# w2 of a mixture-of-experts layer read in runs of 16 KB, its up product at a stride of four, up weights loaded whole

## What is computed

```
h = silu(xb @ w1[e]) * (xb @ w3[e])
out += ((h @ w2[e]) * gate)[rows of the tokens]
```

## Time and profile before

| | before |
|---|---|
| median of 3 runs | 1159.68 us (1159.65 to 1160.03) |
| profiled execution | 1160.26 us |
| its span in the trace | 1158.3 us |
| PE busy | 1002.4 us (87%) |
| DVE busy | 533.9 us (46%) |
| ACT busy | 400.9 us (35%) |
| POOL busy | 273.3 us (24%) |
| moved by DMA | 308.96 MB, mean 267 GB/s |
| weights rawe, 1024 KB loads | 128, median 20.7 us to landing |
| weights rawe, 2048 KB loads | 32, median 25.7 us to landing |

### The profile page before, as it was taken

One profiled execution on the slowest core, in us unless ns is written; L12 is line 12 of the kernel. 1 busy time (PEld: TensorE's weight loads), 2 busy tenths in 40 slices (PEclk: granted clock), 3 DMA queues, 4 the chain that ended last, 5 costly groups with the idle time before them and its releaser, 6 DMA issues. The chain is left out here.

```text
span 1158.3 us, 24709 instructions
## 1 busy us (share of the span) xinstructions
PE 1002.4 (87%) x9068; PEld 695.8 (60%) x9068; DVE 533.9 (46%) x983; ACT 400.9 (35%) x713; POOL 273.3 (24%) x319
## 2 busy tenths in 40 slices
PE   5999999999998999999994789989898888677460
PEld 4888888888886666788884445545454444333230
DVE  5741522111017888655457644352534343434338
ACT  5412233212125667303213334252343434242322
POOL 0101010101000000000000346464555454614120
PEclk9999999999999999999996799999999999989795
DMA  8733331531324004537549999999999999999986
GB/s 317 285 124 119 118 127 45 209 144 45 145 78 169 1 1 146 162 116 308 220 180 401 404 403 414 414 416 414 413 412 414 415 415 413 415 417 415 416 356 244
DMA packets 78645, 308.96 MB, mean 267 GB/s; under 512 B 9400, under 2 KB 9576, under 8 KB 62224
## 3 DMA queue, kind: packets, MB, share of 16 engines
q1 hardware_dynamic: 66224, 273.87, 60.0%
q0 software_dynamic: 12384, 34.63, 7.7%
HBM read 275.68 MB, written 36.44 MB: 269 GB/s over the span
## 5 line engine op out<-in xcount | busy, mean ns | idle before, releaser
L620 PE MATMUL ps<-whi,xTh 128*128 128x512 f32 x480 | 187.6, 391 | 13.9 <-DVE wlo L1283 13.9
L622 PE MATMUL ps<-whi,xTl 128*128 128x512 f32 x480 | 187.5, 391 | 0.0
L621 PE MATMUL ps<-wlo,xTh 128*128 128x512 f32 x480 | 187.5, 391 | 0.0
L915 PE MATMUL ps<-cur13a,xT 128*32 128x256 f32 x1984 | 133.8, 415 | 3.4 <-issue 2.2
L915 PE MATMUL ps<-cur13b,xT 128*32 128x256 f32 x1984 | 121.1, 385 | 13.4 <-DVEq L1780 13.4
L939 PE MATMUL ps<-cur,hT 128*32 128x256 f32 x1952 | 117.9, 382 | 7.5 <-issue 7.5
L1769 DVE COPY cur13a<-rawe 128x4096 f32 x31 | 71.2, 2296 | 112.9 <-DMA rawe<-in_w 63.3
L1017 ACT ACTIVATE zst<-ps,rstd 128x512 f32<-128x512 f32 x60 | 40.8, 688 | 205.0 <-PE ps L622 202.9
L1898 POOL DMA_INDIRECT y_scratch<-ystage,idxs x62 | 88.7, 1431 | 97.0 <-ACT ystage L1225 72.8
L1246 ACT ACTIVATE cur<-rawe 128x4096 f32 x30 | 108.7, 3622 | 8.4 <-issue 7.7
L620 PEld LDWEIGHTS ps<-whi,xTh 128*128 128x128 f32 x480 | 90.6, 189 | 32.7 <-issue 13.9
(11 more groups left out here) (238 smaller groups left out, 1362.4 us busy)
## 6 DMA issues: line engine op xcount, KB each, us to landing
rawe<-in_w SPq DMA_DIRECT2D x128, 1024.0 KB, 20.7
rawe<-in_w SPq DMA_DIRECT2D x32, 2048.0 KB, 25.7
raw<-in_w_in SPq DMA_DIRECT2D x20, 1024.0 KB, 8.0
z_scratch<-zst POOLq DMA_DIRECT2D x60, 256.0 KB, 2.3
gat<-z_scratch SPq DMA_DIRECT2D x12, 512.0 KB, 3.9
xn_scratch<-rrow POOLq DMA_DIRECT2D x6, 1024.0 KB, 5.7
raw<-in_w_out SPq DMA_DIRECT2D x4, 1024.0 KB, 6.7
xcol<-in_x_cols SPq DMA_DIRECT2D x6, 512.0 KB, 10.2
```

The lines of the kernel that those rows point to most:

```text
L620: pe.matmul(out, ah, bh, start=first, stop=False)
L621: pe.matmul(out, ah, bl, start=False, stop=False)
L622: return pe.matmul(out, al, bh, start=False, stop=last)
L915: mm = pe.matmul(ps[0][u * CAP:(u + 1) * CAP, 0:256], xT[:, c % 2, x:x + CAP], cur13[h][:, :, c * 512 + u * P:c * 512 + (u + 1) * P], star ...
```

## The change

w2 is dealt to the partitions as w1 and w3 are: partition p takes the four neighbouring rows 4p to 4p + 3, one run of 16 KB. The hidden units have to follow: chunk u of the hidden must hold the units u, u + 4, u + 8 and so on. So column tile u of the up product reads every fourth column of the weights from column u on, at a stride of four elements (16 bytes), where it read 128 neighbouring ones.

The halves of w1 and w3 are no longer loaded by themselves. Each of the two matrices comes in one load of 2 MB, w1 with `s_w1` and w3 with `s_w3`, and they lie in the slot one after the other, 16 KB each. SP waits until both halves of the slot are copied out, issues w1 and w3, waits for the copy of w2 and issues w2: three loads an expert, where there were five. DVE waits for w1 and w3 ahead of the first copy. A copy still takes half h of both, now from two pieces 16 KB apart in the slot. The hand-issued loads at the start follow, with w1 whole where half 0 of w1 and w3 was.

```diff
--- before.py
+++ after.py
@@ -341,8 +341,8 @@
         s_tbm = sem("s_tbm")
         s_ic = sem("s_ic")
         s_nb = sem("s_nb")
-        s_wa = [sem(f"s_wa{s}") for s in range(RING)]
-        s_wb = [sem(f"s_wb{s}") for s in range(RING)]
+        s_w1 = [sem(f"s_w1{s}") for s in range(RING)]
+        s_w3 = [sem(f"s_w3{s}") for s in range(RING)]
         s_w2 = [sem(f"s_w2{s}") for s in range(RING)]
         s_c13 = sem("s_c13")
         s_cw2 = sem("s_cw2")
@@ -384,7 +384,7 @@
         w_out = A["w_out"][0].rearrange("(p c) n -> p c n", c=KC)
         w_pab = [A[n][0].rearrange("(h p) n -> p h n", p=P) for n in ("w_pa", "w_pb")]
         e_w = [A[n][0].rearrange("e (p h c) f -> e p h (c f)", h=2, p=P) for n in ("w1", "w3")]
-        e_w.append(A["w2"][0].rearrange("e (c p) n -> e p c n", p=P))
+        e_w.append(A["w2"][0].rearrange("e (p c) n -> e p (c n)", c=4))
 
         def expert_of(eng, b):
             return eng.value_load(served[0:1, bass.ds(b, 1)], min_val=0, max_val=NE)
@@ -525,37 +525,30 @@
             sp.dma_start(wrt[:, :, :], A["router_w"].rearrange("(p c) n -> p c n", c=KC)).then_inc(s_rp, 16)
             sp.dma_start(brt[:, :], A["router_b"].rearrange("(a n) -> a n", a=1).partition_broadcast(P)[:, 0, :]).then_inc(s_rp, 16)
             sp.dma_start(gcol[:, :], A["ffn_norm_g"][0].rearrange("(p c) -> p c", c=KC)).then_inc(s_rp, 16)
-            def up_half(x, slot, h):
-
-                for k in range(2):
-                    c = slot * EW + (2 * h + k) * PIECE
-                    sp.dma_start(rawe[:, c:c + PIECE],
-                                 e_w[k][bass.ds(x, 1)][0][:, h, :]).then_inc((s_wa, s_wb)[h][slot], 16)
-
-            def down_weight(x, slot):
-
-                c = slot * EW + 4 * PIECE
-                sp.dma_start(rawe[:, c:c + 2 * PIECE].rearrange("p (h n) -> p h n", h=4),
-                             e_w[2][bass.ds(x, 1)][0]).then_inc(s_w2[slot], 16)
+            def weight(x, slot, k, done):
+                c = slot * EW + k * 2 * PIECE
+                if k < 2:
+                    sp.dma_start(rawe[:, c:c + 2 * PIECE].rearrange("p (h n) -> p h n", h=2),
+                                 e_w[k][bass.ds(x, 1)][0]).then_inc(done[slot], 16)
+                else:
+                    sp.dma_start(rawe[:, c:c + 2 * PIECE], e_w[2][bass.ds(x, 1)][0]).then_inc(done[slot], 16)
 
             def expert(p, x, slot=None):
 
                 held = not isinstance(p, int) or p >= RING
                 slot = p % RING if slot is None else slot
                 if held:
-                    sp.wait_ge(s_c13, 2 if isinstance(p, int) and p == RING else 2 * p - (2 * RING - 1))
-                up_half(x, slot, 0)
-                if held:
                     sp.wait_ge(s_c13, 2 * p - (2 * RING - 2))
-                up_half(x, slot, 1)
+                weight(x, slot, 0, s_w1)
+                weight(x, slot, 1, s_w3)
                 if held:
                     sp.wait_ge(s_cw2, p - (RING - 1))
-                down_weight(x, slot)
+                weight(x, slot, 2, s_w2)
 
             def x2_out(t):
                 sp.dma_start(x2_d[t * P:(t + 1) * P, :], x2[t % 3][:, :]).then_inc(s_x2s[t % 3], 16)
-            for k, n in ((s_wa, 32), (s_wb, 32), (s_w2, 16)):
-                sp.sem_inc(k[2], n)
+            for k in (s_w1, s_w3, s_w2):
+                sp.sem_inc(k[2], 16)
 
             def residual(t):
                 sp.dma_start(xres[t % 3][:, :], x_tiles[t]).then_inc(s_xr[t % 3], 16)
@@ -569,17 +562,17 @@
                 if t < 3:
                     residual(t + 3)
             sp.wait_ge(s_w, 2 * NT - 2)
-            down_weight(EPG * ORDER[1], 1)
-            up_half(EPG * ORDER[2], 2, 0)
+            weight(EPG * ORDER[1], 1, 2, s_w2)
+            weight(EPG * ORDER[2], 2, 0, s_w1)
             sp.wait_ge(s_x2, X2_DONE[NT - 2])
             x2_out(NT - 2)
             sp.wait_ge(s_x2, X2_DONE[NT - 1])
             x2_out(NT - 1)
-            up_half(EPG * ORDER[1], 1, 0)
-            up_half(EPG * ORDER[1], 1, 1)
-            up_half(EPG * ORDER[2], 2, 1)
+            weight(EPG * ORDER[1], 1, 0, s_w1)
+            weight(EPG * ORDER[1], 1, 1, s_w3)
+            weight(EPG * ORDER[2], 2, 1, s_w3)
             sp.wait_ge(s_rr, NT)
-            down_weight(EPG * ORDER[2], 2)
+            weight(EPG * ORDER[2], 2, 2, s_w2)
             expert(3, EPG * ORDER[3])
 
             def number(p):
@@ -913,7 +906,7 @@
                         x = (2 * h + c // 2) * CAP
                         for u in range(NQ):
                             mm = pe.matmul(ps[0][u * CAP:(u + 1) * CAP, 0:256], xT[:, c % 2, x:x + CAP],
-                                           cur13[h][:, :, c * 512 + u * P:c * 512 + (u + 1) * P],
+                                           cur13[h][:, :, c * 512 + u:(c + 1) * 512:4],
                                            start=(h == 0 and c == 0), stop=(h == 1 and c == 3))
                     mm.then_inc((s_13a, s_13)[h], 1)
 
@@ -1182,9 +1175,10 @@
             route_copy(NT - 1)
 
             def first_up(h):
-                act.wait_ge((s_wa, s_wb)[h][0], 32)
-                act.activation(cur13[h][:, :, :], rawe[:, 2 * h * PIECE:(2 * h + 2) * PIECE]
-                               .rearrange("p (k n) -> p k n", k=2), ACT.Copy).then_inc(s_c13, 1)
+                act.activation(cur13[h][:, :, :], rawe[:, 0:4 * PIECE].rearrange("p (k n) -> p k n", k=2)
+                               [:, :, h * PIECE:(h + 1) * PIECE], ACT.Copy).then_inc(s_c13, 1)
+            act.wait_ge(s_w1[0], 16)
+            act.wait_ge(s_w3[0], 16)
             first_up(1)
             act.wait_ge(s_lg, NT)
             act.wait_ge(s_rr, NT)
@@ -1760,15 +1754,16 @@
 
                 def take(h):
 
-                    landed = (s_wa, s_wb)[h]
-                    dve.wait_ge(landed[0], 32 * (e1 // 3) + 32)
-                    dve.wait_ge(landed[1], 32 * ((e1 + 2) // 3))
-                    dve.wait_ge(landed[2], 32 * ((e1 + 1) // 3) + 32)
+                    pair = rawe[:, bass.ds((e1 % RING) * EW, 4 * PIECE)].rearrange("p (k n) -> p k n", k=2)
                     dve.wait_ge((s_13a, s_13)[h], b + 1)
-                    half = rawe[:, bass.ds((e1 % RING) * EW + 2 * h * PIECE, 2 * PIECE)]
-                    dve.tensor_copy(cur13[h][:, :, :], half.rearrange("p (k n) -> p k n", k=2)).then_inc(s_c13, 1)
+                    dve.tensor_copy(cur13[h][:, :, :], pair[:, :, h * PIECE:(h + 1) * PIECE]).then_inc(s_c13, 1)
 
                 with dve.If(e1 > e):
+
+                    for k in (s_w1, s_w3):
+                        dve.wait_ge(k[0], 16 * (e1 // 3) + 16)
+                        dve.wait_ge(k[1], 16 * ((e1 + 2) // 3))
+                        dve.wait_ge(k[2], 16 * ((e1 + 1) // 3) + 16)
                     take(0)
                 dve.wait_ge(s_c13, 2 * e1 + 1)
                 dve.sem_inc(s_ga, 1)
```

## The result

| | before | after |
|---|---|---|
| median | 1159.86 us (4 runs) | 1294.55 us (4 runs, 1291.70 to 1299.04) |
| ratio | | 1.1156 (95% interval 1.1140 to 1.1172) |
| profiled execution, span | 1160.26, 1158.3 us | 1299.04, 1297.1 us |
| PE busy | 1002.4 us | 1218.5 us |

The change makes the kernel 134.7 us slower. The forecast was 1156.8 us with a range up to 1162.0; what came is the rival called *The stride costs*, which had 0.18.

What follows compares the result with a forecast made beforehand. The prediction took the full DMA rings to bound the expert stage, with PE close behind. 1160.26 - 4.6 + 0 + 0.2 + 1.5 = 1157.4 us, put at 1156.8 because the profiled execution lay 0.6 above the median; range 1152.0 to 1162.0.

Steps and rivals of the forecast that it cites:

- The stride costs: Strided moving columns in the up product take longer: 1187 us at ratio 1.33, +138 us at double pace; chance 0.18.
- What bounds the kernel: Expert stage, 700 to 1000 us: the 16 DMA rings are full at 414 GB/s, PE idle for only 27.6 us.
- Part 1: w2's loads in runs of 16 KB instead of 4 KB: 4.6 us less, between 3.7 and 5.5.
- The step from 4 to 8 KB: w2's loads at the 8 KB packet rate instead of 4 KB: 0.136 us less each, 3.7 us over 27 experts.
- Part 2: Up product on PE reading columns at a stride of four: no cost, bounded by the loads' ratio of 1.33.
- Part 3: Up weights in two whole 2 MB loads, taken as 8 KB packets; changed waits cost 0.2 plus 1.5 us.
- the first rival: Up loads' two 8 KB runs merge into 16 KB packets: 3.7 us less again, 1153.1 us; chance 0.13.
- (a): SP holds w1 until both halves are copied; early gap moves from 664 to about 655 us: 0.2 us more, bounds 0 to 1.6.
- (b): DVE's first copy waits for whole w1 and w3, delaying the last scatter: 1.5 us more, bounds 0 to 4.5.
- (c): POOL's gathers wait behind 16 KB packets, 0.61 us instead of 0.16, but are fetched two blocks ahead: nothing.
- the merged rival: Up loads go out as 16 KB packets as well, 3.7 us less again: 1153.1 us; chance 0.13.

Runs made afterwards that it cites:

- w2 alone: The kernel before with only w2 read in runs of 16 KB, up product on neighbouring columns and old waits kept: 1154.34 us, ratio 0.9945.

## Why the prediction was wrong

**What bounds the kernel** held: the DMA rings, with PE 27.6 us behind in 300. This small room is what the stride broke.

**Part 1** held: 4.6 us were taken, 6.4 (4.4 to 8.2) measured, so that the term lies within the interval, near its low end. The plateau with w2 alone is 418 GB/s, as the forecast said; (1 - 414/418) x 410 = 3.9 us by it. The step from 4 to 8 KB was met closely (3.7 and 3.6).

**Part 2** is the step that failed. It priced the stride at nothing, and it cost 1.88 us a half (3.63 - 1.75), in all 134.7 + 9.5 = 144 us between the changed kernel and the same one with neighbouring columns (each against its own before). The working took its price from *stationary* loads: eight strided transposes keep the pace of eight contiguous ones, so the stride seemed free. But what is read at a stride of eight there is a stationary block, loaded beside the running product, and the up product reads the *moving* operand at a stride. The longer single load, 189 against 142 ns, seemed to point the right way, but it is no clean sign of a stride. Line 620 loads 128 neighbouring columns, and before's page has 189 ns for it too:

```profile
L620 PEld LDWEIGHTS ps<-whi,xTh 128*128 128x128 f32 x480 | 90.6, 189 | 32.7 <-issue 13.9
```

Its ratio of 1.33 was also too small: measured is 3.63/1.75 = 2.07. The bound at the other end was drawn from this row as if it were an end; no row of before showed a strided moving operand, so it wasn't one.

The rival took double the pace and gave +138 us, against 134.7. That agreement is partly luck. It counted only the 43 blocks of 700 to 1000. All 62 at 3.89 us are 241 us, of which the span shows 216.1 as busy time, and 77.3 of these were paid by idling. Most of the 25 missing from the 241 can be read. The busy time of the up product alone grew less than the starts: before, 2756 of its records in 700 to 1000 take 164.3 us, 3.81 us for the 64 records of a block, and after, 1936 take 227.3, 7.52 a block. That is 3.70 us more, not 3.89, which makes some 12 us over 62 blocks. And before, part of the stage ran at a lower granted clock: a block took 4.70 us in 1000 to 1112 (648 records, 47.6 us, clock 0.85) and 4.15 in 640 to 700 (512, 33.2 us, clock 0.92), together some 12 us above 3.81.

The Trainium skill (Advanced Engine Details and Errata, section Memory Cachelines) says that at least two accesses to a 16-byte line are wanted, and that a new line at each access costs. The prediction let the pace of eight speak against it. The traces agree with this for the moving operand: two columns a line cost 0.1 us a half, one a line doubles it.

**Part 3** took 8 KB packets for the up loads; they merged to 16 KB, as the first rival said (8,192 packets fewer). (a) With neighbouring columns the gap moved from 664 to 655 as worked out: 652 to 658 loses (1 - 269/414) x 6 = 2.1 us, and 664 to 668 nothing, in place of 1.6. That is +0.5, where +0.2 was taken. (b) The scatter took ye's place as said: it costs 2.6 and 3.0 us at the issue of ya, of which 1.0 and 1.4 are left at the end, where 1.5 was taken and 4.5 was the bound. The size was met, but not for the reason given. No gain from draining rings is seen (5.5 us from the last scatter to ya, where 5 were counted); the chain behind ya, taken as fixed at some 29 us, took 27.7. (c) Nothing speaks against the zero for the gathers, and no run separates it.

With the stride put aside, the merged rival's sum was -4.6 - 3.7 + 0.2 + 1.5 = -6.6 us; the experiment with neighbouring columns gave -9.5 (-7.5 to -11.4). The rings gave more than the sum had: 9.7 us by the plateau, less 0.5 and 1.0, make 8.2.

## What to carry to other kernels

Price an access pattern by rows of the same operand: a stationary load says nothing of the moving operand, and where the trace has no row of it, the far bound has to be set by what would turn the bound of the stage, here anything over 17%. When a layout is chosen for the DMA, look at what it makes the matrix product read: two neighbouring fp32 columns a step (w2 in two runs of 8 KB) kept most of the gain (8.4 of 9.5 us), while the stride that one run of 16 KB asks for cost 15 times what all the longer runs gave (144 against 9.5). And an engine at half load need not be a free place for the stride: DVE's sorting copy, which stands in the chain of a block, made the kernel 5% slower than before.

## What the runs showed of the hardware

- The PE's moving operand in fp32: 0.83 to 0.85 ns a column without a stride, 1.77 to 1.84 ns for each new 16-byte line with one; halves of 1.75, 1.85, 2.75, 3.63 and 3.68 us for strides of 1, 2, 3, 4 and 8. Four column tiles side by side pay no more each than one alone (1.77 ns).
- Loads of the stationary operand, 128x128: 142 ns in the transposes without a stride and 189 in those with a stride of eight, but also 189 for neighbouring columns in line 620; so the length of a single load doesn't tell a stride.
- DVE's copy of 4096 fp32 a partition, reading at a stride of four: 4.05 us instead of 2.29, 0.99 ns an element.
- Two neighbouring runs of 8 KB, written as two pieces on both sides, went as packets of 16 KB, and runs of 16 KB carried the stage at 424 GB/s (4 KB for w2 and 8 KB for the rest: 414).
